# The convolution's layer norm and the first output products moved between the steps of the last pair of heads

## The chip, the cores and the metric

The kernel runs on one core of a Trainium2 chip. The metric is the device time of one launch in microseconds (us); the median of several runs counts. The profile is one more execution, taken by the hardware profiler.

## The reference

The program is two blocks on x of 512 tokens by 2048 channels, all in f32. Only the first half of the first block touches the change:

```python
u = rms_norm(h, norm_mix)
proj = u @ w_in                      # conv val, conv gate, r, k, v, three small ranks
y_conv = conformer_conv(val, gate, ...)   # val*sigmoid(gate), 31 causal taps, layer_norm over 1024, silu
y_rwkv = rwkv7_time_mix(...)         # 16 heads of 64, recurrent state, per-head norm, gate
mixed = concatenate([y_conv, y_rwkv])
h = h + mixed @ w_out                # 2048 x 2048
v = rms_norm(h, norm_ffn)
h = h + hierarchical_moe(v, ...)     # router, 32 experts, top 2
```

A second block (windowed attention beside a state-space layer) follows. Neither it nor the experts are edited.

## The kernel before

**Layout.** Activations lie transposed: 128 channels in the partitions, 512 tokens along the row. A "unit" is one product of 128 channels by 512 tokens. For the input projection a unit is 16 "steps", one matmul each over a block of 128 input channels (`DenseOne.step`). There are 43 of them, `N_IN`: one `lora`, two `rank`, and eight each of `val`, `gate`, `r`, `k` and `v`, in the order of `UNITS_ONE`, which is `FIRST` and then `LATER`. They take turns in two PSUM banks; a unit starts when ScalarE has evicted the one two before it. Weights come in panels of two units into a ring of two slots (`DenseOne.load`, on SyncE's queue SP).

**The pairs.** The time mix runs over eight pairs of heads, `pair(j)` on every engine. A pair has chunks of 64 tokens. TensorE makes masked scores, inverts a triangular system in five levels (`level_w`, `level_t`, each with an eviction on VectorE and copies on ScalarE between), forms the chunk transfers and then goes through six state steps. Its work is cut into 23 slots (`SLOTS_ONE`: A0 to A2, L0 to L4b for the levels, H, M, F, S1 to S6 for the state steps, and Y). Behind the small products of each slot TensorE takes as many projection steps as a table says: `FULL_SHARE` (sum 80) for pairs 0 to 5, `LAST_SHARE` (sum 64) for pair 6, none for pair 7. 9 units (`FIRST`) come ahead of pair 0. ScalarE evicts a finished unit in the same slot (`units(name)`), VectorE mixes it with the token before in the next one (`mix`), and GpSimd multiplies val by the gate (`gate_units`).

**The convolution.** VectorE takes a tile of 128 channels in 32 instructions (31 taps and one addition). How many of them stand in each slot is in `CONV_SHARE`, for each tile that the pair has: one tile in pairs 1 to 5, tiles 5 and 6 in pair 6, tile 7 in pair 7.

**The norm and the output.** After pair 7 TensorE sums the eight tiles over channels with `ones` (L764), VectorE centres them (L1251), ScalarE squares (L942), TensorE sums the squares (L769), VectorE and ScalarE form the reciprocal root, VectorE scales (L956), ScalarE applies Silu with gain and bias (L947). Then come 16 output units of 8 matmuls each (`out_unit`, L263) with the convolution's half of `w_out`, four panels of four units (one unit for each block of 128 tokens), which VectorE adds to the rows of x. The last pair's own norm (`mean`, `centre`, `variance`, `var`, `flip_y`, `norm_y`, `finish_y`) lies between them, and `pair_done` reaches 8 when it is through. `Middle` follows: 16 units with the other half of `w_out` (L1414), whose panels are the "late" ones, and the router in the same loop. The experts' weights then stream through a ring of 16 chunks of 1 MB; seven chunks are asked for early.

**SyncE's queue, in order:** output panels 0 and 1; rows of x after all 43 units; `c_scaled`; late panels 0 and 1; output panel 2; the router's inputs and seven expert chunks after `pair_done`; output panel 3; late panels 2 and 3.

## Time and profile before

| | us |
|---|---|
| median of 3 runs (3897.91 to 3901.66) | 3897.92 |
| profiled execution | 3898.68 |
| its span | 3896.7 |

| stretch of the span, us | what runs |
|---|---|
| 41 to 174 | units ahead of pair 0 |
| 174 to 979 | pairs 0 to 6 |
| 979 to 1041 | pair 7 |
| 1041 to 1071 | the convolution's norm |
| 1071 to 1184 | 16 output units of the convolution's half |
| 1184 to 1338 | the other half of the output, the router |
| 1338 to 2320 | experts |
| 2320 to 3897 | the second block |

The span is the time from the first to the last instruction; the execution has 2.0 us more around it. "PEclk" or the granted clock is the share of TensorE's full 2.4 GHz that it was given: 1.00 is 2.4 GHz and 0.50 is 1.2 GHz. PE is TensorE, DVE VectorE, ACT ScalarE, POOL GpSimd, SP SyncE.

### The profile page before, as it was taken

How to read it: one execution, taken by the hardware profiler on the slowest of the kernel's cores; microseconds unless marked ns; L12 is line 12 of the kernel's file. 1: busy time of each engine (PE TensorE's matmuls, PEld its weight loads, DVE VectorE, ACT ScalarE, POOL GpSimd, SP SyncE). 2: the span in 40 equal slices, each digit the busy share in tenths (PEclk: the TensorE clock that was granted, in tenths of full speed). 3: DMA queues.
4: the chain of work that ended last, by engine and by line, in shares of the span. 5: the costliest groups of instructions: out<-in, count | busy, mean ns of one | idle time of the engine just before them, and what ended most of it. 6: DMA issues, size and time to landing. Idle time of an engine off the chain costs nothing. (4 is left out here: it accounts for less than half of the span.)

```text
span 3896.7 us, 48147 instructions
## 1 busy us (share of the span) xinstructions
PE 3577.4 (92%) x20413; PEld 2129.6 (55%) x20413; DVE 1256.8 (32%) x2316; ACT 537.0 (14%) x976; POOL 415.1 (11%) x404
## 2 busy tenths in 40 slices
PE   8999999999699887777777768999999999999999
PEld 4455555555445432232322227754446888888888
DVE  2325445457511200000000004436302355444442
ACT  2122221222201100000000004110011010331000
POOL 0000000000000000000000000003020000465511
PEclk9999999999899899999999989999999999999999
DMA  4211111220151499999999987322443322222432
GB/s 116 65 46 44 46 46 46 56 58 23 68 184 44 194 421 422 422 422 422 421 420 419 417 340 192 104 81 87 108 113 108 114 85 67 76 83 103 162 117 77
DMA packets 318685, 666.31 MB, mean 171 GB/s; under 512 B 42972, under 2 KB 227718, under 8 KB 265125
## 3 DMA queue, kind: packets, MB, share of 16 engines
q1 hardware_dynamic: 310693, 636.35, 44.9%
q0 software_dynamic: 7808, 27.28, 1.9%
q8 instruction: 143, 2.34, 0.2%
q14 instruction: 41, 0.34, 0.0%
HBM read 636.44 MB, written 43.91 MB: 175 GB/s over the span
## 5 line engine op out<-in xcount | busy, mean ns | idle before, releaser
L1781 PE MATMUL experts_run_bank<-whole_big 128*64 128x512 f32 x2048 | 491.3, 627 | 169.1 <-DMA whole_big<-in_expert_w_gate 100.8
L2304 PE MATMUL stream_bank<-whole_big 128*128 128x256 f32 x2912 | 638.4, 380 | 0.6 <-DVE whole_big L3406 0.6
L242 PE MATMUL first_bank<-whole_big 128*128 128x512 f32 x1344 | 637.0, 611 | 1.3 <-PEq L80 1.3
L2304 PEld LDWEIGHTS stream_bank<-whole_big 128*128 128x128 f32 x2912 | 551.6, 190 | 80.0 <-issue 3.7
L2209 PE MATMUL stream_bank<-whole_big 128*128 128x512 f32 x1024 | 443.9, 593 | 0.0
L1781 PEld LDWEIGHTS experts_run_bank<-whole_big 128*64 128x64 f32 x2048 | 169.8, 144 | 489.7 <-issue 489.5
L242 PEld LDWEIGHTS first_bank<-whole_big 128*128 128x128 f32 x1344 | 241.5, 191 | 263.8 <-issue 253.1
L2209 PEld LDWEIGHTS stream_bank<-whole_big 128*128 128x128 f32 x1024 | 193.0, 190 | 236.4 <-issue 235.9
L1801 PE MATMUL experts_run_bank<-whole_big 128*64 128x512 f32 x1024 | 230.0, 596 | 35.2 <-DMA whole_big<-in_expert_w_down 22.8
L1846 DVE TENSOR_TENSOR whole_big<-whole_big,experts_run_bank 128x512 f32<-128x512 f32 x16 | 11.0, 687 | 650.2 <-PE experts_run_bank L1781 650.2
L2355 DVE TENSOR_TENSOR whole_big<-stream_bank,whole_big 128x256 f32<-128x256 f32 x250 | 102.2, 422 | 330.8 <-PE stream_bank L2304 330.8
L2947 PE MATMUL stream_bank<-whole_big 128*128 128x256 f32 x896 | 193.5, 379 | 0.0
L2947 PEld LDWEIGHTS stream_bank<-whole_big 128*128 128x128 f32 x896 | 170.2, 190 | 23.1
L1801 PEld LDWEIGHTS experts_run_bank<-whole_big 128*64 128x64 f32 x1024 | 79.1, 137 | 175.0 <-issue 167.1
L1022 DVE SCALAR_TENSOR_TENSOR whole_big<-whole_big 128x512 f32<-128x512 f32 x232 | 174.1, 785 | 0.2
L956 DVE TENSOR_TENSOR whole_big<-first_bank,whole_big 128x512 f32<-128x512 f32 x88 | 59.2, 688 | 291.1 <-PE first_bank L563 163.8
L956 DVE TENSOR_TENSOR whole_big<-whole_big 128x512 f32<-128x512 f32 (+3 forms) x158 | 113.2, 743 | 103.9 <-ACT whole_big L797 41.2
L263 PE MATMUL first_bank<-whole_big 128*128 128x512 f32 x256 | 112.8, 603 | 10.5 <-ACT whole_big L947 10.5
L1289 POOL TENSOR_TENSOR whole_big<-whole_big 128x512 f32<-128x512 f32 x40 | 54.5, 1375 | 634.1 <-DVE whole_big L956 491.0
L1414 PE MATMUL first_bank<-whole_big 128*128 128x512 f32 x256 | 113.4, 596 | 0.0
L2207 PE MATMUL stream_bank<-whole_big 128*128 128x256 f32 x512 | 111.7, 379 | 1.4 <-issue 1.4
L2207 PEld LDWEIGHTS stream_bank<-whole_big 128*128 128x128 f32 x512 | 96.7, 190 | 14.4 <-issue 1.6
(465 smaller groups left out, 3184.6 us busy)
## 6 DMA issues: line engine op xcount, KB each, us to landing
whole_big<-in_expert_w_gate SPq DMA_DIRECT2D x128, 1024.0 KB, 27.2
whole_big<-in_expert_w_up SPq DMA_DIRECT2D x128, 1024.0 KB, 30.0
whole_big<-in_expert_w_down SPq DMA_DIRECT2D x128, 1024.0 KB, 26.9
whole_big<-in_w_in SPq DMA_DIRECT2D x110, 1024.0 KB, 7.7
whole_big<-in_w_out SPq DMA_DIRECT2D x16, 1024.0 KB, 7.3
whole_big<-in_w_out SPq DMA_DIRECT2D x8, 2048.0 KB, 12.7
gates_two<-whole_big SPq DMA_DIRECT2D x40, 256.0 KB, 7.8
whole_big<-gates_two POOLq DMA_DIRECT2D x40, 256.0 KB, 3.0
```

The costliest lines, as they stand in the source:

```text
L242: mm = pe.matmul(bank[:, :], slot[:, k, sub * P:(sub + 1) * P], u_T[:, k, :], start=(k == 0), stop=(k == KD - 1))
L263: mm = pe.matmul(bank[:, :], mixed_T[:, k, token * P:(token + 1) * P], wide[:, k, :], start=(k == 0), stop=(k == 7))
L956: tt = lambda out, x, z, op: dve.tensor_tensor(out, x, z, op)
L1022: conv.did(dve.scalar_tensor_tensor(out=acc, in0=at, scalar=w, in1=acc, op0=ALU.mult, op1=ALU.add))
L1414: mm = pe.matmul(bank[:, :], self.mixed_T[:, 8 + k, t * P:(t + 1) * P], self.late[cb][:, k, :], start=(k == 0), stop=(k == 7))
L1781: mm = pe.matmul(bank[self.half(h), :], self.x_T[:, PARTS * q + k, self.half(h)], self.ring[slot][:, k, :], start=(q == 0 and k == 0), sto ...
L1801: mm = pe.matmul(self.y_bank[q][self.half(h), :], self.hidden_T[:, k, self.half(h)], self.ring[slot][:, q, :], start=(k == 0), stop=(k == ...
L2207: mm = pe.matmul(bank[:, 0:PW], left[:, k, t * P:(t + 1) * P], slot[:, k, :], start=(k == 0), stop=(k == KD - 1))
L2209: mm = pe.matmul(bank[:, :], slot[:, k, (u % 2) * P:(u % 2 + 1) * P], left[:, k, :], start=(k == 0), stop=(k == KD - 1))
L2304: mm = pe.matmul(self.place[m % 3], weights[:, k, :], left[:, k, :], start=(k == 0), stop=(k == self.k - 1))
L2355: ins = dve.tensor_tensor(to, bank, other, ALU.add)
L2947: mm = pe.matmul(out_place[q % 6], left[:, k, j * P:(j + 1) * P], right[:, k, :], start=(k == 0), stop=(k == 7))
```

## The change

- `FIRST` has one more unit, (val, 0): 10 units ahead of pair 0. The order in `LATER` is new: from pair 0 on, units finish as k, v, gate, val, r. All gates are through in pair 6's slot L2, v 7 in its S2. `LAST_SHARE` sums to 48.
- The convolution's tiles: 0 and 1 in pair 1, one each in pairs 2 to 5, 6 and 7 in pair 6, none in pair 7.
- In pair 7, `CLOSE_SHARE` says how many steps of a new kind (`close`) TensorE takes in each slot, 76 in all: 8 sum products in A0, 8 products of squares in L0 and L0b, and from L3 on 60 output matmuls, four in each slot and eight in Y. The other 68 output matmuls come after the pair.
- VectorE centres tiles in A1 and A2, forms variance in L0b and reciprocal in L1, scales in L1b and L2; ScalarE squares in A1 and L0, takes the root in L0b, and applies Silu in L2 and L2b. Both sums use the banks of the projection in place of R[0] and R[1], and there are three buffers for squares in place of two.
- VectorE adds output units 0 to 5 to the rows within the pair. The last pair's own norm lies between output units 7 to 11.
- SyncE: the rows of x after output panel 1 as before; output panel 2; then `c_scaled` and all of `y_mm`; late panels 0 and 1; output panel 3; then the router's inputs and the seven expert chunks.

```diff
-FIRST = [("lora", 0), ("rank", 0), ("rank", 1), ("r", 0), ("k", 0), ("v", 0), ("v", 1), ("r", 1), ("k", 1)]
...
+FIRST = [("lora", 0), ("rank", 0), ("rank", 1), ("r", 0), ("k", 0), ("v", 0), ("v", 1), ("r", 1), ("k", 1), ("val", 0)]
+LATER = [("gate", 0), ("val", 1), ("gate", 1), ("val", 2), ("r", 2)]
+LATER += [unit for j in range(2, 7) for unit in (("k", j), ("v", j), ("gate", j), ("val", j + 1), ("r", j + 1))]
+LATER += [("k", 7), ("gate", 7), ("v", 7)]
...
+SUM_U, VAR_U, OUT_U = N_IN, N_IN + 1, N_IN + 2
...
-LAST_SHARE = (5, 4, 4, 5, 5, 4, 5, 3, 2, 3, 2, 2, 2, 2, 2, 2, 1, 1, 1, 1, 1, 1, 6)
+LAST_SHARE = (5, 4, 4, 4, 4, 3, 4, 4, 3, 2, 2, 1, 1, 1, 1, 1, 2, 2, 0, 0, 0, 0, 0)
+CLOSE_SHARE = (8, 0, 0, 4, 4, 0, 0, 0, 0, 4, 4, 4, 4, 4, 4, 4, 4, 4, 4, 4, 4, 4, 8)
...
+CONV_CENTRES = {"A1": range(0, 4), "A2": range(4, 8)}
+CONV_SQUARES = {"A1": range(0, 3), "L0": range(3, 8)}
+CONV_VAR, CONV_ROOT, CONV_FLIP = "L0b", "L0b", "L1"
+CONV_SCALES = {"L1b": range(0, 4), "L2": range(4, 8)}
+CONV_SOFT = {"L2": range(0, 4), "L2b": range(4, 8)}
...
+    def out_step(self, pe, mixed_T):
+
+
+        u, k = self.at, self.k
         panel = panel_of_one(u)
-        slot, use, token = self.ring[panel % 2], panel // 2, (u - N_IN) % 4
+        slot, use, token = self.ring[panel % 2], panel // 2, (u - OUT_U) % 4
         wide = slot[:, :, :].rearrange("p (k two) c -> p k (two c)", two=2)
         bank = self.bank[u % 2]
-        pe.wait_ge(self.bank_free[u % 2], u // 2)
-        for k in range(8):
-            if token == 0 and k % 4 == 0:
-                pe.wait_ge(self.arrived[panel % 2][k // 4], 16 * use + 16)
-            mm = pe.matmul(bank[:, :], mixed_T[:, k, token * P:(token + 1) * P], wide[:, k, :], start=(k == 0), stop=(k == 7))
-        mm.then_inc(self.product, 1)
+        if k == 0:
+            self.open(pe, u)
+        if token == 0 and k % 4 == 0:
+            pe.wait_ge(self.arrived[panel % 2][k // 4], 16 * use + 16)
+        mm = pe.matmul(bank[:, :], mixed_T[:, k, token * P:(token + 1) * P], wide[:, k, :], start=(k == 0), stop=(k == 7))
+        self.k += 1
+        if self.k == 8:
+            mm.then_inc(self.product, 1)
+            self.at, self.k = u + 1, 0
...
-        squares = [kk, k2]
-        conv_var, conv_rstd = rate, e_inv
+        squares = [kk, k2, key_tmp]
+        conv_var, conv_rstd = rate, change
...
-                    if panel == PANELS_IN + 2:
-                        middle.sync_early(sp)
                     if panel == PANELS_IN + 1:
                         sp.wait_ge(dense.product, N_IN)
                         sp.dma_start(rows[:, :, :], a["x"][0].rearrange("(t p) d -> p t d", p=P)).then_inc(sem["rows_in"], 16)
+                    if panel == PANELS_IN + 2:
                         sp.wait_ge(sem["c_scaled"], CT)
+                        sp.wait_ge(sem["y_mm"], CT)
                         middle.sync_late(sp, 0)
                         middle.sync_late(sp, 1)
+                middle.sync_early(sp)
                 middle.sync(sp)
...
+                def close():
+
+
+                    n = closed[0]
+                    closed[0] = n + 1
+                    i = n % CT
+                    if n < CT:
+                        wait("conv", 32 * (n + 1))
+                        if i == 0:
+                            dense.open(pe, SUM_U)
+                        mm = pe.matmul(dense.bank[SUM_U % 2][:, :], ones[:, :], mixed_T[:, i, :], start=(i == 0), stop=(i == CT - 1))
+                        if i == CT - 1:
+                            mm.then_inc(dense.product, 1)
+                    elif n < 2 * CT:
+                        if i == 0:
+                            dense.open(pe, VAR_U)
+                        wait("c_sq", i + 1)
+                        mm = pe.matmul(dense.bank[VAR_U % 2][:, :], ones[:, :], squares[i % 3], start=(i == 0), stop=(i == CT - 1))
+                        mm.then_inc(*((sem["c_var_mm"], 1) if i < CT - 1 else (dense.product, 1)))
+                    else:
+                        if n == 2 * CT:
+                            dense.at = OUT_U
+                            wait("c_done", CT)
+                        dense.out_step(pe, mixed_T)
...
-                    after = share(j)
...
-                        dense.fill(pe, u_T, n)
+                        if more:
+                            dense.fill(pe, u_T, n)
+                        else:
+                            for _ in range(n):
+                                close()
...
+                dense.fill(pe, u_T, KD)
                 for j in range(CT):
                     pair(j)
-                wait("conv", 32 * CT)
-                wait("mt_ev", CT)
-                for i in range(CT):
-                    mm = pe.matmul(R[0][:, :], ones[:, :], mixed_T[:, i, :], start=(i == 0), stop=(i == CT - 1))
...
+                close_to(out_left + 1)
                 mean(CT - 1)
-                wait("c_done", CT)
-                for i in range(16):
-                    dense.out_unit(pe, N_IN + i, mixed_T)
-                    if i == 1:
-                        variance(CT - 1)
+                close_to(out_left + 3)
+                variance(CT - 1)
+                close_to(OUT_U + 16)
...
+                def square_conv(i):
+                    wait("c_centred", i + 1)
+                    if i >= 3:
+                        wait("c_var_mm", i - 2)
+                    act.activation(squares[i % 3], mixed_T[:, i, :], ACT.Square).then_inc(sem["c_sq"], 1)
+
+                def root_conv():
+                    wait("c_var", 1)
+                    act.activation(conv_var, conv_var, ACT.Sqrt).then_inc(sem["c_root"], 1)
+
+                def soft_conv(i):
+                    wait("c_scaled", i + 1)
+                    act.activation(mixed_T[:, i, :], mixed_T[:, i, :], ACT.Silu, bias=cols["conv_ln_b"][:, i:i + 1],
+                                   scale=cols["conv_ln_g"][:, i:i + 1]).then_inc(sem["c_done"], 1)
...
+                        if not more and name in CONV_SQUARES:
+                            for i in CONV_SQUARES[name]:
+                                square_conv(i)
+                        if not more and name in CONV_SOFT:
+                            for i in CONV_SOFT[name]:
+                                soft_conv(i)
+                        if not more and name == CONV_ROOT:
+                            root_conv()
...
+                def centre_conv(i):
+                    bank = dense.done(dve, SUM_U)
+                    ins = dve.scalar_tensor_tensor(out=mixed_T[:, i, :], in0=bank[:, :], scalar=-1.0 / n_conv, in1=mixed_T[:, i, :],
+                                                   op0=ALU.mult, op1=ALU.add)
+                    ins.then_inc(sem["c_centred"], 1)
+                    if i == CT - 1:
+                        wait("c_centred", CT)
+                        dve.sem_inc(dense.bank_free[SUM_U % 2], 1)
+
+                def var_conv():
+                    bank = dense.done(dve, VAR_U)
+                    dve.tensor_scalar(conv_var, bank[:, :], 1.0 / n_conv, 1e-5, ALU.mult, ALU.add).then_inc(sem["c_var"], 1)
+                    wait("c_var", 1)
+                    dve.sem_inc(dense.bank_free[VAR_U % 2], 1)
+
+                def flip_conv():
+                    wait("c_root", 1)
+                    dve.reciprocal(conv_rstd, conv_var).then_inc(sem["c_flipped"], 1)
+                    wait("c_flipped", 1)
+
+                def scale_conv(i):
+                    tt(mixed_T[:, i, :], mixed_T[:, i, :], conv_rstd, ALU.mult).then_inc(sem["c_scaled"], 1)
+
+                def add_row(i):
+                    bank = dense.done(dve, OUT_U + i)
+                    if i == 0:
+                        wait("rows_in", 16)
+                    at = rows[:, i % 4, (i // 4) * T:(i // 4 + 1) * T]
+                    tt(at, at, bank[:, :], ALU.add).then_inc(dense.bank_free[(OUT_U + i) % 2], 1)
...
-                    tiles = ([], [0], [1], [2], [3], [4], [5, 6], [7])[j]
+                    tiles = ([], [0, 1], [2], [3], [4], [5], [6, 7], [])[j]
...
+                        if more:
+                            return
+                        if i:
+                            for u in out_finished(i - 1):
+                                add_row(u)
+                        for k in CONV_CENTRES.get(name, ()):
+                            centre_conv(k)
+                        if name == CONV_VAR:
+                            var_conv()
+                        if name == CONV_FLIP:
+                            flip_conv()
+                        for k in CONV_SCALES.get(name, ()):
+                            scale_conv(k)
...
+                left = out_finished(len(SLOTS_ONE) - 1)[0]
+                for i in range(left, 16):
+                    if i == left + 1:
+                        centre(CT - 1)
+                    if i == left + 4:
                         var(CT - 1)
-                    if i == 4:
+                    if i == left + 5:
                         flip_y(CT - 1)
-                    if i == 5:
                         norm_y(CT - 1)
                         finish_y(CT - 1)
                         middle.vector_early(dve)
+                    add_row(i)
```

## Rows read from the trace of the kernel before

**Rows 1.** The page: busy time of each engine, and the group of the convolution's taps.

```profile
PE 3577.4 (92%) x20413; PEld 2129.6 (55%) x20413; DVE 1256.8 (32%) x2316; ACT 537.0 (14%) x976; POOL 415.1 (11%) x404
...
L1022 DVE SCALAR_TENSOR_TENSOR whole_big<-whole_big 128x512 f32<-128x512 f32 x232 | 174.1, 785 | 0.2
```

**Rows 2.** Stretches: length, busy PE, PEld, DVE, ACT, POOL; granted clock, DMA share, GB/s.

```profile
748.00:864.00 116.00, 116.00 (x1134) 62.39 (x1134) 58.84 (x82) 27.74 (x40) 7.95 (x6) 1.00 0.15 38
...
864.00:979.00 115.00, 110.81 (x1104) 60.17 (x1103) 78.39 (x114) 25.74 (x38) 8.45 (x6) 0.93 0.13 39
...
979.00:1041.00 62.00, 44.02 (x962) 38.70 (x960) 41.44 (x59) 13.06 (x21) 8.11 (x6) 0.84 0.27 103
...
1041.00:1071.00 30.00, 17.98 (x39) 6.88 (x36) 14.44 (x19) 13.61 (x20) 0.00 (x0) 0.84 0.02 2
...
1071.00:1184.00 113.00, 113.00 (x258) 49.77 (x258) 16.42 (x22) 2.09 (x3) 0.78 (x4) 0.98 0.44 161
...
1338.00:2320.00 982.00, 770.32 (x3392) 292.15 (x3392) 73.43 (x112) 39.50 (x65) 36.72 (x61) 0.96 0.99 412
```

**Rows 3.** Waits of TensorE, 864 to 1184 us: total, times, longest.

```profile
PE first_bank L590 <- DVE whole_big L956: 12.4, 4, 4.5
...
PE first_bank L263 <- ACT whole_big L947: 10.5, 1, 10.5
...
PE first_bank L734 <- DVE whole_big L1124: 6.9, 9, 1.3
```

**Rows 4.** Timeline of TensorE: start, duration, what, records.

```profile
159.31 13.89 PE L242 MATMUL first_bank<-whole_big 128*128 128x512 f32 x32
...
382.56 1.98 PE L242 MATMUL first_bank<-whole_big 128*128 128x512 f32 x4
...
403.40 1.15 PE L563 MATMUL first_bank<-whole_big 64*64 64x64 f32 x32
...
865.64 1.15 PE L563 MATMUL first_bank<-whole_big 64*64 64x64 f32 x32
...
974.77 4.68 PE L242 MATMUL first_bank<-whole_big 128*128 128x512 f32 x8
...
979.37 2.36 PE L563 MATMUL first_bank<-whole_big 64*64 64x64 f32 x64
...
990.81 1.97 PE L590 MATMUL first_bank<-whole_big 64*64 64x64 f32 x32 [4.55 <-DVE whole_big L956]
...
1087.90 96.29 PE L263 MATMUL first_bank<-whole_big 128*128 128x512 f32 x224
...
1184.03 6.17 PE L1414 MATMUL first_bank<-whole_big 128*128 128x512 f32 x14
```

**Rows 5.** Timeline of VectorE in pair 6.

```profile
905.89 1.29 DVE L956 TENSOR_TENSOR whole_big<-first_bank,whole_big 128x512 f32<-128x512 f32 x2 [4.38 <-PE first_bank L563]
...
932.62 0.69 DVE L956 TENSOR_TENSOR whole_big<-first_bank,whole_big 128x512 f32<-128x512 f32 x1 [1.70 <-PE first_bank L579]
...
949.65 0.23 DVE L1121 COPY whole_big<-first_bank 128x64 f32<-128x64 f32 x1 [1.36 <-PE first_bank L724]
...
963.64 0.28 DVE L1124 SCALAR_TENSOR_TENSOR whole_big<-whole_big,first_bank 128x64 f32<-128x64 f32 x1
```

**Rows 6.** Stretches of 4 us, columns as in rows 2.

```profile
960.00:964.00 4.00, 3.67 (x11) 1.58 (x12) 4.00 (x10) 0.00 (x0) 0.00 (x0) 0.50 0.00 0
...
1044.00:1048.00 4.00, 4.00 (x9) 1.75 (x9) 0.00 (x0) 0.00 (x0) 0.00 (x0) 0.87 0.00 0
```

**Rows 7.** Timeline of VectorE and ScalarE in the norm.

```profile
1060.80 3.35 DVE L1256 RECIPROCAL whole_big<-whole_big 128x512 f32<-128x512 f32 x1 [0.69 <-ACT whole_big L944]
...
1064.18 4.92 DVE L956 TENSOR_TENSOR whole_big<-whole_big 128x512 f32<-128x512 f32 x8
...
1064.91 5.75 ACT L947 ACTIVATE whole_big<-whole_big,whole_one 128x512 f32<-128x512 f32 x8 [2.85 <-DVE whole_big L956]
```

**Rows 8.** Timeline of SP's queue.

```profile
1118.74 0.37 SPq L1380 DMA_DIRECT2D whole_big<-in_router_group_w  x1
```

More of the change, by code:

```diff
@@ L156, in finished, with out_finished @@
     return range(done // KD, (done + share(j)[slot]) // KD)
+def out_finished(slot):
+    done = sum(CLOSE_SHARE[:slot]) - 2 * CT
+    return range(max(done, 0) // 8, max(done + CLOSE_SHARE[slot], 0) // 8)
 def panel_of_one(u):
-    return 0 if u < 2 else 1 + (u - 3) // 2 if u < N_IN else 1 + (N_IN - 3) // 2 + (u - N_IN) // 4
+    return 0 if u < 2 else 1 + (u - 3) // 2 if u < N_IN else 1 + (N_IN - 3) // 2 + (u - OUT_U) // 4
+CONV_CENTRES = {"A1": range(0, 4), "A2": range(4, 8)}
[3 more added lines that the diff above has]
+CONV_SOFT = {"L2": range(0, 4), "L2b": range(4, 8)}
 PANELS_IN = panel_of_one(N_IN - 1) + 1
@@ L517, in _ @@
                     dense.load(sp, panel)
-                    if nearest < CT and panel < PANELS_IN and dense.last(panel - 2) >= len(FIRST) + 5 * (nearest - 2) + 3:
+                    if nearest < CT and panel < PANELS_IN and dense.last(panel - 2) >= len(FIRST) + 5 * (nearest - 2) + 2:
                         load_up(nearest)
                         nearest += 1
-                    if panel == PANELS_IN + 2:
-                        middle.sync_early(sp)
                     if panel == PANELS_IN + 1:
@@ L603, in variance @@
                     pe.matmul(R[5][:, :], block_ones[:, :], tmp, start=True, stop=True).then_inc(sem["var_mm"], 1)
+                closed = [0]
+                def close():
[20 more added lines that the diff above has]
+                        dense.out_step(pe, mixed_T)
                 def pair(j):
                     more = j < CT - 1
-                    after = share(j)
+                    after = share(j) if more else CLOSE_SHARE
                     spent = {}
@@ L758, in _, with close_to @@
                 bonus_sum(0)
+                dense.fill(pe, u_T, KD)
                 for j in range(CT):
                     pair(j)
[L761 to L776 removed]
+                def close_to(u):
+                    while dense.at < u:
+                        close()
+                close_to(out_left + 1)
+                mean(CT - 1)
+                close_to(out_left + 3)
+                variance(CT - 1)
+                close_to(OUT_U + 16)
                 wait("pair_done", CT)
@@ L1365, in unit @@
     def unit(self, i):
-        return N_IN + 16 + i
+        return OUT_U + 16 + i
     def sync_late(self, sp, i):
@@ L1387, in sync @@
         sem, dense = self.sem, self.dense
-        sp.wait_ge(dense.product, N_IN + 12)
+        sp.wait_ge(dense.product, OUT_U + 12)
         self.sync_late(sp, 2)
-        sp.wait_ge(dense.product, N_IN + 16)
+        sp.wait_ge(dense.product, OUT_U + 16)
         self.sync_late(sp, 3)
@@ L1682, in gpsimd @@
                            pattern=[[1, P]], channel_multiplier=-1).then_inc(sem["counted"], 1)
-        pool.wait_ge(self.dense.product, N_IN + 32)
+        pool.wait_ge(self.dense.product, OUT_U + 32)
         pool.memset(self.expert.x, 0.0).then_inc(sem["x_clear"], 1)
```

55 lines of the change are left out of this document (9 added, 46 removed).

## Prediction

> **What bounds the kernel now.** I read the page first: TensorE is busy 92% of the span, so what can be won is its idle time and the time it spends at half clock [rows 1]. The table of stretches then says where that is [rows 2]. From 748 to 864 us (the pair of heads before the last two) TensorE is busy 116.00 of 116.00 us at a granted clock of 1.00 (2.4 GHz). The trouble lies in 864 to 1071: pair 6 is at clock 0.93; the last pair (979 to 1041) is busy for 44.02 of 62.00 us at 0.84; in the convolution's norm (1041 to 1071) it is busy 17.98 of 30.00. The output products behind (1071 to 1184) are full again. The waits of TensorE from 864 to 1184 name the causes [rows 3]: 12.4 us for VectorE's evictions of the levels, 10.5 for ScalarE's Silu before the first output product, 6.9 for VectorE's state steps. So up to 1184 TensorE's own order sets the time. Behind it come the router and then the experts, which move 412 GB/s at a DMA share of 0.99 [rows 2]; that stream waits for ring slots which TensorE's first expert products free, so what TensorE wins before it starts, the stream wins too.
>
> **Prices.** A matmul of 512 columns is two records: 16 projection steps took 13.89 us back to back (from 159.31), 0.87 each, and 112 output steps took 96.1 us (1087.90 to 1184.03), 0.86 each [rows 4]. Four whole pairs from 403.40 to 865.64 give 115.6 us each. Of that 80 steps take 69.6 and the small products 46.0; the last pair lacks the next pair's ranks and sums (about 6), so its own work is 39.3 us at full clock. It lasted 61.7 (from 979.37 to just behind 1041), and from its start to the router's first product (1184.03) it is 204.7 us.
>
> **Part 1: one more projection unit ahead of pair 0** (FIRST has 10 units): +13.9 us. Nothing hides it: TensorE had no wait there to fill. The sizes for pairs 0 to 5 stay at 80 steps each, only the kinds of unit change places. The gates now come at L4b, each with a table load on ScalarE; it falls into the time of the fill, cost 0.
>
> **Part 2: pair 1 takes two convolution tiles instead of one.** Pair 6 shows what two tiles do: VectorE is busy 78.39 us of 115, against 58.84 of 116 with one tile in pair 5 [rows 2]. With full fills that fits everywhere but in the six state steps: VectorE needs 14.0 us for them with two tiles (949.65 to 963.64 [rows 5]), 2.3 each, and TensorE's own rhythm there is 2.2, two fills of 1.98 (from 382.56 [rows 4]) and 0.2 of small products. I take +1 us; the bounds are 0 and 5 (a spell at half clock).
>
> **Part 3: pair 6 has 48 fills instead of 64.** 16 steps are 13.9 us if TensorE sets the pace. It doesn't throughout. Up to the rb/rk masks (905.89) VectorE has idle time, and three steps fewer bring them 2.7 us forward. From there to the first state copy (949.65) VectorE idles 1.70 us before 932.62, 1.36 before 949.65 and little else in 43.8 [rows 5]. The last eviction of the levels (932.62) comes 3.2 us sooner; then 13.1 us of VectorE work, two taps and the q sum stand in a row, and state copy 0 comes 4.6 us sooner where TensorE alone would give 7.0. The six state steps are VectorE's (949.65 to 963.64 with no idle), and the mixing of v 7 now stands among them, +1.3: the last is 3.3 sooner. Then the six fills of slot Y are gone: they ran at or near half clock, 2.0 for each of two and 4.6 for the last four (from 974.77) [rows 4, 6], less 0.6 for waits that they covered. Together -11.4 us (period 102.3). Bounds: -7 and -14.5.
>
> **Part 4: the last pair and the norm.** Taken away: the 32 taps in it, 25 us at 0.785 each [rows 1], and the serial norm behind it. Added between its steps: 8 sum products, 8 variance products, 60 output steps. I count from the pair's start. The clock is half there, since waits in the state steps bring it down (before: 0.50 from 960 on [rows 6]). Scores 4.0, sum products 9.9 (about 4 us of them at half clock, as the norm's sum needed, which began at 1041: 0.87 from 1044 on [rows 6]): 13.9. Turns, scores, y's mean and level 0's product: 18.4. VectorE has meanwhile 8 centrings at 0.61 (as its 8 scalings took [rows 7]), a mask, y's centring and the eviction: 20.8, hidden by 4 variance products (21.9). Squaring 2.2, turns 1.0, y's variance 1.0, four more variance products with 0.3 of waiting for squares: 29.9. Level 1 with 1.0 of wait: 34.2. Scores and level 2's product: 38.1. Here comes the wait that takes the place of the old one: VectorE does the norm's reciprocal (3.35) to 35.3, the masks to 38.3, y's reciprocal (3.35), four scalings at 0.61 and the eviction, until 44.7. TensorE waits 6.7 us with nothing to fill (L1b has share 0); before, the longest such wait was 4.5 [rows 3]. Then 4.4 of products to 49.3, and ScalarE has four Silus left after X's copy (0.72 each [rows 7]) until 51.9; output steps wait for all eight, so 2.7 more: 52.1. From L3 on every slot has 4 steps, which cover everything (in pairs 0 to 5, 2 to 4 steps did). Left: own work 16.6 and 60 steps at 0.86, 51.5: 120.2. Behind: 68 steps 58.3, y's mean and variance 2.0: 180.5. After the two long waits I add 4.0 for half clock, for behind the old wait of 4.55 us (990.81) 32 small products took 1.97 us instead of the 1.1 of full clock, and the rest of their run with them [rows 4]. 184.5 against 204.7: -20.2 us. Bounds: no half clock and half the waits, 171; half clock to L3, 203.
>
> **Part 5: the queues.** SP asks for x's rows when the 43 units are done, now in pair 6; for output panel 2 four units into the output; then it waits for y_mm of the last pair, asks for late panels 0 and 1 (4 MB, 10 us at the experts' 412 GB/s), needed 8.5 units, 58 us, later. Output panel 3 stands behind them, needed 28 us after its slot frees. Router inputs and seven expert chunks come after pair_done, which falls some 28 us before the output ends (before 66, at 1118.74 [rows 8]). The chunks are 7.3 MB, 18 us; late panel 2 stands behind them and lands about when the output ends, 14 us before its use; late panel 3 is asked for as before. The router's weights have some 40 us. Cost 0; without that cover, the late panel would cost what exceeds 14.
>
> **Sum.** 13.9 + 1 - 11.4 - 20.2 = -16.7 us. The profiled execution took 3898.7 (span 3896.7, 2.0 around it), 0.8 above the median of 3897.9; 3897.9 - 16.7 = 3881.2, so 3881.
>
> **The rivals.**
> (B) The waits are smaller than walked: pair 6 sheds all 16 steps (-14.0), pair 1 costs nothing, the 9.4 us of new waits halve and no half clock follows them (-28.9): 13.9 - 14.0 - 28.9 = -29, 3870. For it: I took each engine's work as coming in one piece after its last input, where some of it can start sooner. Against: two reciprocals and the masks in a row on VectorE between level 1 and level 2.
> (C) VectorE sets pair 6: it has 79.7 us of work and the levels' round trips, and sheds 3 us instead of 11.4. The unit moved ahead is paid twice: 3881 + 8.4 = 3889 to 3890. For it: the full row of VectorE's work before the state steps [rows 5]. Against: the Y fills stand behind that work.
> (D) Slower: half clock holds on in the last pair. At 960 it fell to 0.50 though TensorE was busy 3.67 of 4.00 us, with single steps between small products [rows 6], and the last pair still began near it. In the new last pair, slots A1 to L2b are small products between waits. At half clock up to L3 its 37 us of work cost up to 19 more than I counted: 3900. It decides whether the clock is still half where L3 begins, for then the slots L3 to H (34 us of work) run so too: 3930, slower. Against: in the row from 1044 it was back at 0.87, some 4 us after dense products began, and the sum products are dense, as are the runs of four steps from L3 on. The Trainium skill (TensorE: Matmul & The Clock Gate, "HAM oscillation — how this bites in real kernels") says that waits between short bursts of matmuls bring the clock down again and again; the fall in the row at 960 agrees. By that rule alone each of the two new waits would be followed by a cold stretch, and the kernel would come out near 3900.
> (E) The change wins on TensorE but not at the end: late panel 2, the router's weights or x's rows arrive late and give back what was won, 3893 to 3898. Against: the margins of part 5.
>
> **How the numbers follow.** A (as summed, 3874 to 3889) 0.55; B 0.20; C 0.12; D 0.06; E 0.07. The bound for "no change" is 0.2%, 7.8 us, which is about what a measurement of this kernel can tell: below 3890.1 is faster. That takes A, B and 0.05 of C: 0.80; same 0.14; slower 0.06. The range 3865 to 3893 leaves out D, E and the edge of B.
>
> **What would show it.** Pair 0 starts at about 188 instead of 174. Pair 6 lasts about 102 us, with TensorE waiting for state steps longer than before (6.9 us with the last pair's [rows 3]). The last pair starts near 983 and ends near 1103; its longest wait is a level-2 eviction of 6 to 7 us, and there is none before the output products but 3 us for Silu. The router's first product comes at about 1167 instead of 1184, and from there every stage is as long as before. I am wrong if pair 6 lasts over 106 us (C), if the clock of the last pair before L3 is under 0.7 (D), or if the way from 1184 to the first expert product (154 us) has grown (E).

## The result and the profile after

| | before | after |
|---|---|---|
| median, us | 3897.92 (5 runs, 3892.96 to 3901.66) | 3877.25 (5 runs, 3875.67 to 3880.40) |
| ratio, 95% interval | | 0.9950 (0.9937 to 0.9963) |
| profiled execution, span | 3898.68, 3896.7 | 3875.67, 3873.9 |

The change makes the kernel 20.7 us faster, where -16.7 was forecast; 3877 lies in the range of 3865 to 3893. In a second job, with six runs, the changed kernel gave 3878.2, ratio 0.9954 (0.9943 to 0.9966).

The page of the changed kernel: busy time, and the group of the output steps (L283, before L263), whose waits were 10.5 us in [rows 3].

```profile
PE 3567.3 (92%) x20413; PEld 2123.0 (55%) x20413; DVE 1263.4 (33%) x2316; ACT 539.1 (14%) x978; POOL 419.0 (11%) x404
...
L283 PE MATMUL first_bank<-whole_big 128*128 128x512 f32 x256 | 116.4, 605 | 2.6 <-ACT whole_big L911 2.6
```

The stretches, columns as in rows 2: pair 1 with two tiles, pair 6, the last pair with what is between its steps, the experts.

```profile
283.00:399.00 116.00, 115.91 (x1134) 62.38 (x1133) 75.00 (x106) 26.46 (x39) 8.05 (x6) 1.00 0.16 42
...
877.00:978.00 101.00, 90.17 (x1061) 53.02 (x1062) 80.89 (x116) 23.75 (x36) 9.03 (x6) 0.93 0.20 75
978.00:1099.00 121.00, 111.21 (x1121) 64.00 (x1118) 37.40 (x52) 24.31 (x39) 6.76 (x5) 0.92 0.09 30
...
1315.00:2297.00 982.00, 769.61 (x3392) 292.67 (x3392) 73.43 (x112) 39.50 (x65) 36.56 (x61) 0.96 0.99 412
```

Pair 1 is still busy 115.91 of 116 us. Pair 6 is 101 us long and not 115, but TensorE is busy only 90.17 of them. The separate stretch for the norm is gone. The experts' 982 us are as long as before [rows 2], so what was won ahead of them stayed won.

The timeline of TensorE: the unit ahead of pair 0, the starts of pair 0, pair 6 and the last pair, its sum products and what follows them, the two long waits and the router's first product.

```profile
171.32 13.89 PE L255 MATMUL first_bank<-whole_big 128*128 128x512 f32 x32
185.15 1.15 PE L588 MATMUL first_bank<-whole_big 64*64 64x64 f32 x32
...
876.97 1.15 PE L588 MATMUL first_bank<-whole_big 64*64 64x64 f32 x32
...
978.24 0.36 PE L588 MATMUL first_bank<-whole_big 64*64 64x64 f32 x1
...
984.20 8.23 PE L642 MATMUL first_bank<-whole_big,whole_ones 128*128 128x512 f32 x14
992.27 1.04 PE L593 MATMUL first_bank<-whole_ident,whole_big 128*128 128x128 f32 x8
...
1021.08 1.97 PE L615 MATMUL first_bank<-whole_big 64*64 64x64 f32 x32 [6.27 <-DVE whole_big L1019]
...
1029.69 5.10 PE L283 MATMUL first_bank<-whole_big 128*128 128x512 f32 x8 [2.58 <-ACT whole_big L911]
...
1161.29 13.90 PE L1506 MATMUL first_bank<-whole_big 128*128 128x512 f32 x32
```

| from, to | before [rows 4] | after | difference | forecast |
|---|---|---|---|---|
| extra unit ahead of pair 0 | | 13.83 (171.32 to 185.15) | +13.8 | +13.9 |
| pair 0 to pair 6 | 691.65 | 691.82 | +0.2 | +1 |
| pair 6 to last pair | 113.73 | 101.27 | -12.5 | -11.4 |
| last pair to router | 204.66 | 183.05 | -21.6 | -20.2 |
| sum | | | -20.1 | -16.7 |

The router's first product comes 22.7 us sooner, since another 2.6 us lie in the opening, which the change doesn't touch. Of the runs of 32 transposes there, the second took this long before and after (timeline of TensorE in each kernel):

```profile
20.43 5.47 PE L418 MATMUL opening_bank<-whole_big 128*128 128x128 f32 x32 [1.84 <-DVE whole_big L388]
```

```profile
19.48 3.84 PE L441 MATMUL opening_bank<-whole_big 128*128 128x128 f32 x32 [1.84 <-DVE whole_big L411]
```

In the twelve further profiles below, all of kernels that are the same as the changed one up to there, pair 0 starts between 185.16 and 187.96 us. So the difference is chance of one execution. The end has such chance too: from the experts' first product to the end of the span, the changed kernel took 2558.1 us in this profile (from 1315.85 to 3873.9) and 2562.3 in its second one (after_again). So what follows is read from the stretches and not from the span, and medians that differ by some 4 us or less are not told apart by themselves.

The waits of TensorE from 877 to 1160 us; L615 is the eviction wait of the levels and L790 that of the state steps, in rows 3 L590 and L734 (1.1 us more for a state copy stand at y's first product, L798):

```profile
PE first_bank L615 <- DVE whole_big L1019: 7.1, 2, 6.3
PE first_bank L790 <- DVE whole_big L1219: 6.7, 3, 3.8
PE first_bank L790 <- DVE whole_big L1216: 2.9, 1, 2.9
PE first_bank L283 <- ACT whole_big L911: 2.6, 1, 2.6
```

The long one, 6.27 us at level 2 (1021.08), is VectorE's work in a row. In its timeline the norm's reciprocal (1009.50), the two masks, y's reciprocal, four scalings and then the eviction (1020.35) follow with one pause, 0.68 us for the masks' scores:

```profile
1009.50 3.34 DVE L1191 RECIPROCAL whole_big<-whole_big 128x512 f32<-128x512 f32 x1
1013.53 1.29 DVE L1019 TENSOR_TENSOR whole_big<-first_bank,whole_big 128x512 f32<-128x512 f32 x2 [0.68 <-PE first_bank L588]
1014.74 3.34 DVE L1159 RECIPROCAL whole_big<-whole_big 128x512 f32<-128x512 f32 x1
1018.00 2.43 DVE L1019 TENSOR_TENSOR whole_big<-whole_big 128x512 f32<-128x512 f32 x4
1020.35 0.68 DVE L1019 TENSOR_TENSOR whole_big<-first_bank,whole_big 128x512 f32<-128x512 f32 x1
```

The clock around the pair's start, columns as in rows 6. It was 0.50 from 968 to 988 though TensorE was busy nearly all the time from 976 on; it was back once the sum products (from 984.20) had run for some 4 us:

```profile
972.00:976.00 4.00, 3.19 (x54) 3.03 (x55) 3.97 (x8) 0.00 (x0) 0.00 (x0) 0.50 1.00 414
976.00:980.00 4.00, 3.94 (x75) 3.75 (x73) 0.65 (x1) 0.60 (x1) 0.00 (x0) 0.50 1.02 424
...
984.00:988.00 4.00, 4.00 (x11) 1.82 (x8) 3.87 (x5) 0.00 (x0) 2.95 (x2) 0.50 0.00 0
988.00:992.00 4.00, 4.00 (x10) 1.77 (x10) 0.56 (x1) 0.00 (x0) 0.00 (x0) 0.98 0.00 0
```

SP's queue: late panels 0 and 1, output panel 3, then the router's inputs at 1133.70. No wait of TensorE for a transfer appears in the waits above.

```profile
1096.12 2.19 SPq L1465 DMA_DIRECT2D whole_big<-in_w_out  x4
1104.83 0.92 SPq L231 DMA_DIRECT2D whole_big<-in_w_out  x2
1133.70 0.37 SPq L1472 DMA_DIRECT2D whole_big<-in_router_group_w  x1
```

### The profile page after: what moved, and what is told of

Its sections match the earlier page's. It is cut to its first block and busy times, and to the rows that moved or that the text cites. A ratio compares the mean times of both kernels' runs of the same rounds, so it can differ in the third digit from the quotient of the medians.

```text
span 3873.9 us, 48151 instructions
## 1 busy us (share of the span) xinstructions
PE 3567.3 (92%) x20413; PEld 2123.0 (55%) x20413; DVE 1263.4 (33%) x2316; ACT 539.1 (14%) x978; POOL 419.0 (11%) x404
## 5 line engine op out<-in xcount | busy, mean ns | idle before, releaser
L283 PE MATMUL first_bank<-whole_big 128*128 128x512 f32 x256 | 116.4, 605 | 2.6 <-ACT whole_big L911 2.6
```

The costliest lines, as they stand in the source:

```text
L283: mm = pe.matmul(bank[:, :], mixed_T[:, k, token * P:(token + 1) * P], wide[:, k, :], start=(k == 0), stop=(k == 7))
```

## The experiments

All ratios are to the kernel before in the same job, whose median was 3896.9 to 3899.3 us from job to job. "Pair 6" and "last" are the stretches of the table above in each kernel's own profile.

| kernel | median | ratio, 95% interval | pair 6 | last |
|---|---|---|---|---|
| before | 3897.9 | | 113.7 | 204.7 |
| the changed kernel | 3877.3 | 0.9950 (0.9937 to 0.9963) | 101.3 | 183.1 |
| after_again | 3878.2 | 0.9954 (0.9943 to 0.9966) | 101.3 | 184.6 |
| norm_in_outputs_behind | 3881.4 | 0.9961 (0.9946 to 0.9976) | 101.3 | 185.7 |
| norm_behind_no_taps | 3897.6 | 0.9997 (0.9988 to 1.0007) | 101.4 | 199.7 |
| early_back | 3909.2 | 1.0035 (1.0023 to 1.0046) | 101.3 | 212.7 |
| taps_in_y | 3875.7 | 0.9946 (0.9933 to 0.9959) | 97.4 | 181.1 |
| flip_later | 3874.8 | 0.9937 (0.9924 to 0.9951) | 101.3 | 179.4 |
| warm_steps | 3869.7 | 0.9931 (0.9917 to 0.9944) | 99.0 | 178.7 |
| taps_and_flip | 3871.2 | 0.9927 (0.9914 to 0.9941) | 97.5 | 179.1 |
| warm_steps_flip | 3869.4 | 0.9922 (0.9908 to 0.9935) | 99.2 | 176.8 |
| warm_all_flip | 3866.4 | 0.9921 (0.9907 to 0.9934) | 99.0 | 172.8 |
| warm_all_taps_flip | 3859.5 | 0.9899 (0.9884 to 0.9914) | 93.6 | 172.8 |
| warm_router_too | 3863.0 | 0.9915 (0.9902 to 0.9929) | 93.6 | 172.8 |

**The changed kernel again.** 

> The changed kernel once more, beside the others on the same chip. From the two traces the gain is made of +13.8 us (unit ahead of pair 0), about 0 (pairs 0 to 5), -12.5 (pair 6), -21.6 (last pair to the router), together -20; another 2.6 us of the profiled difference lay in the opening, where one of the two executions had its transposes at half clock for longer. If the opening is chance, the ratio of times is 0.9945 to 0.9952 and the new trace may have either opening; if the change causes the earlier start, every trace of the changed kernel starts pair 0 at 185 us and the gain is 22 to 23.

The ratio, 0.9954, is just outside the 0.9945 to 0.9952 that was expected if the opening is chance, by far less than its interval, and pair 0 started at 187.56 us instead of 185.15. The opening's first four runs of transposes took 6.54, 5.46, 5.46 and 3.84 us, as in the kernel before (6.43, 5.47, 5.47 and 3.84), where the first profile of the changed kernel had 5.25, 3.84, 5.47 and 3.84: it is chance. The last pair's stretch differs by 1.5 us between the two profiles of the same kernel. The spell of half clock behind the wait for Silu is longer in the second one: the granted clock was 0.50 and 0.73 in its two rows from 1032 to 1040 us, and 0.93 and 1.00 in those of the first.

**The outputs behind the pair, the norm within.**

```diff
-CLOSE_SHARE = (8, 0, 0, 4, 4, 0, 0, 0, 0, 4, 4, 4, 4, 4, 4, 4, 4, 4, 4, 4, 4, 4, 8)
+CLOSE_SHARE = (8, 0, 0, 4, 4) + (0,) * 18
...
-                left = out_finished(len(SLOTS_ONE) - 1)[0]
+                left = 0
```

> The 16 sum and variance products stay in the last pair, the 60 output steps go behind it. If the steps in slots L3 to S6 cover waits and keep the clock up, their waits come back as in the kernel before (about 5 us for levels and state steps behind the 2.6 us for Silu) and so does the half clock from the state steps on (some 15 us of it before, 7 lost): slower than the changed kernel by 9 to 13 us, 3886 to 3890. If the norm's place alone makes the gain and the output steps only change places, it is within 3 us of the changed kernel.

A miss. The stretch is 185.7 us, 1.1 to 2.6 longer than in the two profiles of the changed kernel, and the median 3 to 4 higher. The waits do come back, 5.4 us of them behind level 2's eviction, about as expected, and half clock too. But the wait of 2.6 us for Silu is gone, since no output step stands right behind the Silus any more. In its timeline a wait for a level's eviction is 0.80 us, one for a state copy 0.38, and from 1044 on the small products run at half clock (0.48 for four):

```profile
1028.65 1.15 PE L615 MATMUL first_bank<-whole_big 64*64 64x64 f32 x32 [0.80 <-DVE whole_big L1019]
...
1042.68 0.33 PE L790 MATMUL first_bank<-whole_big 64*64 64x64 f32 x4 [0.38 <-DVE whole_big L1219]
...
1048.47 0.48 PE L798 MATMUL first_bank<-whole_big 64*64 64x64 f32 x4
```

So the output steps had only some 3 us net to cover, and a spell of half clock. Against that, the changed kernel starts a run of output steps in each of 14 slots, and each start costs about 0.2 us (eight records take 3.70 us alone, and 3.5 in a long run), an estimated 3 us. This balance is worked out from the traces; no run changes one part of it alone.

**The norm behind the pair too.**

```diff
-CLOSE_SHARE = (8, 0, 0, 4, 4, 0, 0, 0, 0, 4, 4, 4, 4, 4, 4, 4, 4, 4, 4, 4, 4, 4, 8)
+CLOSE_SHARE = (0,) * 23
...
-CONV_CENTRES = {"A1": range(0, 4), "A2": range(4, 8)}
...
+CONV_CENTRES, CONV_SQUARES, CONV_SCALES, CONV_SOFT = {}, {}, {}, {}
+CONV_VAR = CONV_ROOT = CONV_FLIP = None
...
+                for i in range(CT):
+                    centre_conv(i)
+                var_conv()
+                flip_conv()
+                for i in range(CT):
+                    scale_conv(i)
+                left = 0
```

(ScalarE's squares, root and Silus move behind the pair in the same way.)

> Units, tiles and queue as in the changed kernel, but the sum and variance products, the whole norm and all output steps stand behind the last pair. From the pair's start to the router it was 204.7 us before, 183 to 185 after, and 185.7 with only the outputs behind. If the norm's place makes the gain, this kernel pays its serial chain again (26 to 28 us from the pair's end to the first output step) and takes back only the taps that left the last pair (some 12 us of its 62, since the waits for levels and state steps shrink): 192 to 196 us, 3885 to 3891 in all. If the gain came mostly from the taps' departure, it is under 190.

199.7 us, above the 192 to 196 expected, and the whole gain is gone (0.9997). The wait for Silu is back, longer than in [rows 3]:

```profile
PE first_bank L280 <- ACT whole_big L908: 11.3, 1, 11.3
```

With this one the 21.6 us split: 204.7 to 199.7 by the taps leaving the last pair (4.9), 199.7 to 185.7 by the norm between its steps (14.1), 185.7 to 183.1 or 184.6 by the output steps (1.1 to 2.6). The parts were taken in this one order; in another they could share out otherwise. I had expected the taps to give 12.

**Router inputs and expert chunks ahead of output panel 3.**

```diff
                 for panel in range(2, PANELS_IN + 4):
+                    if panel == PANELS_IN + 3:
+                        middle.sync_early(sp)
                     dense.load(sp, panel)
...
-                middle.sync_early(sp)
                 middle.sync(sp)
```

> Router inputs and seven expert chunks are asked for ahead of output panel 3 again, as in the kernel before. In the changed kernel pair_done comes when output unit 12, the first of panel 3, is about to start (1133.7 us). If the order of the queue matters, panel 3 is asked for only then and stands behind 7.3 MB: unit 12 waits 18 to 26 us, 3895 to 3903. If the transfers of several requests run side by side and share the rate, or if the wait is taken back in front of the experts, it costs under 10 us.

The order of the queue matters, and more than expected. TensorE waits 27.4 us for the panel, and the kernel is 31 us slower than the changed one and slower than before. The first reason is that SP itself needs 8 us from the first small request to the panel's, and the second that the panel, asked for at 1144.30, lands at 1163.85 behind 7.3 MB.

```profile
PE first_bank L283 <- DMA whole_big<-in_w_out: 27.4, 1, 27.4
```

```profile
1136.17 0.37 SPq L1473 DMA_DIRECT2D whole_big<-in_router_group_w  x1
...
1144.30 4.21 SPq L231 DMA_DIRECT2D whole_big<-in_w_out  x2
```

So the new order of requests earns nothing that these runs show, but with the output products moved it is needed: before, `pair_done` came at 1118 [rows 8], with more than half of the output units still ahead; now it comes when panel 3 is about to be used.

**16 taps of pair 6 in slot Y of pair 5.**

```diff
+LAST_TAPS = (0, 5, 0, 2, 3, 3, 0, 3, 2, 2, 4, 2, 2, 6, 2, 2, 1, 1, 1, 1, 1, 1, 4)
...
-                        for _ in tiles:
-                            k = (conv.n + 0) // 32
-                            n = CONV_SHARE[i]
+                        counts = [CONV_SHARE[i]] * len(tiles) if j != 6 else [LAST_TAPS[i]]
+                        if j == 5 and name == "Y":
+                            counts.append(16)
+                        for n in counts:
```

> 16 of the 64 taps of pair 6 are done in slot Y of pair 5, where VectorE is idle for some 14 us; six of them come out of the slots before L2b, ten out of those behind, six of these from the state steps. If VectorE sets pair 6 from level 2 to the last state step, as the trace says (TensorE waits 10.7 us there for state copies), pair 6 shortens by 6 to 9 us and the kernel by as much: 3868 to 3871. If the round trips between the engines set it and not VectorE's work, under 2 us.

Between the two: pair 6 is 3.9 us shorter, not 6 to 9, and against 0.9950 and 0.9954 the ratio of 0.9946 is no difference that this measurement can tell. The waits for state copies fell from 10.7 to 7.0 us (below, with 0.5 at y's first product); up to the first state step the pair lost only 0.9 us, from 80.4 to 79.4, though eight taps had left that part and VectorE's busy time in it had fallen by 5.5 us, from 61.3 to 55.8. So VectorE sets the state steps, but the levels of pair 6 seem to be set by both engines in turn. The last stretch, 181.1 us, is shorter too, by 2.0 to 3.5.

```profile
PE first_bank L792 <- DVE whole_big L1221: 4.5, 3, 3.1
PE first_bank L792 <- DVE whole_big L1218: 2.0, 1, 2.0
```

**y's reciprocal behind level 2's eviction.**

```diff
-                    if j:
+                    if j and more:
                         flip_y(j - 1)
...
-                    if j:
+                    if j and more:
                         norm_y(j - 1)
                     rest("L2")
+                    if not more:
+                        flip_y(j - 1)
+                        norm_y(j - 1)
```

> In the last pair the reciprocal and norm of the pair before (y) come behind level 2's eviction and the scalings, no longer ahead of it. The walk through the pair says that the wait at level 2 (6.3 us) is VectorE's serial work between two handoffs, of which this reciprocal is 3.35: the wait falls to about 3, the Silu wait stays at 2.6, and the half clock behind the wait shortens: 3 to 6 us faster than the changed kernel. If the wait had another cause (the masks' scores, or the copies of ScalarE), nothing changes; if the Silus set the start of L3 anyway, the gain is taken back by a longer wait there.

The stretch is 3.7 to 5.2 us shorter and the median 2.4 to 3.4 lower: the reciprocal was part of the wait. The wait fell to 4.2 and not to 3, and that for Silu stayed, as expected.

```profile
PE first_bank L615 <- DVE whole_big L1019: 4.9, 2, 4.2
PE first_bank L283 <- ACT whole_big L911: 2.6, 1, 2.6
```

**Unused matmuls in pair 6's waits.** They read finished data, and their sums are never used; the output is unchanged.

```diff
                         fill(f"S{c}")
+                        if j == CT - 2:
+                            for _ in range({3: 1, 4: 4, 5: 1, 6: 1}.get(c, 0)):
+                                pe.matmul(R[4][:, :], block_ones[:, :], K_in[1][:, 1:1 + T], start=True, stop=True)
```

> Seven matmuls of 512 columns whose results nobody uses stand in slots S3 to S6 of pair 6, where TensorE waits for state copies. They are extra work, 6.1 us at full clock, laid into 7.8 us of waits. If half clock is what makes the end of pair 6 and the start of the last pair slow (0.50 from 968 to 988 us), the clock stays near 1.00 and y's products, scores and the first sum products get some 6 to 8 us back: 3869 to 3873. If the clock doesn't follow from these waits, or falls anyway, the kernel is the same or up to 3 us slower.

As the first case of the expectation says. TensorE has 14 more instructions (two records for each matmul), and the kernel is faster: the two stretches are 6.6 to 8.2 us shorter together, and the median 7.5 to 8.5 lower, though the intervals of the ratios overlap. The clock is 1.00 in each row where it was 0.50 above (columns as in rows 6), and the waits are filled:

```profile
968.00:972.00 4.00, 3.12 (x14) 1.09 (x14) 4.00 (x8) 0.00 (x0) 0.00 (x0) 1.00 1.06 408
...
976.00:980.00 4.00, 4.00 (x91) 3.06 (x87) 1.60 (x3) 0.60 (x1) 0.00 (x0) 1.00 1.01 418
...
984.00:988.00 4.00, 3.93 (x45) 2.56 (x43) 2.44 (x5) 1.59 (x4) 0.00 (x0) 1.00 0.02 4
```

```profile
PE first_bank L790 <- DVE whole_big L1219: 2.9, 1, 2.9
PE first_bank L790 <- DVE whole_big L1222: 0.9, 2, 0.7
```

Pair 6 is 2.2 us shorter (y's products at full clock), and the last pair 4.4 to 5.9. Its scores and sum products show it directly: they took 14.03 us in the changed kernel (978.24 to 992.27), and 9.38 here, from 976.39 to the next line:

```profile
985.77 1.04 PE L593 MATMUL first_bank<-whole_ident,whole_big 128*128 128x128 f32 x8
```

**Both rearrangements.** The edits of taps_in_y and flip_later.

> Both rearrangements, taps in Y and the later reciprocal, in one kernel. They act in different pairs, so the gains add: 9 to 14 us on the changed kernel, 3863 to 3868. If either gain only moves TensorE's wait to the other place, the sum is that of one.

3871.2, 6 to 7 us under the changed kernel, less than the 9 to 14 expected. In the trace the gains don't add fully: 97.5 for pair 6 as with the taps alone, and 179.1 for the rest, as with the later reciprocal alone. The 2.0 to 3.5 us by which the taps alone had shortened the last stretch don't come on top; why, wasn't tried.

**The later reciprocal and the unused matmuls.** The edits of flip_later and warm_steps.

> The seven unused matmuls in pair 6 and the later reciprocal in the last pair. Alone they gave 2.3 us in pair 6 with 4.4 to 6 from the last pair's start, and 3.6 in the last pair. They act on different waits: the last pair to the router takes 175 to 176 us against 183 to 185, the kernel 3865 to 3867.

The stretch is 176.8, somewhat more than the 175 to 176 expected and a further 1.8 us under warm_steps; the median (3869.4, 3865.6 to 3870.3) can't be told from that of warm_steps alone. Against flip_later, which differs only by the seven unused matmuls, the two stretches are 2.1 and 2.5 us shorter and the median is 5.4 lower.

**Unused matmuls in the last pair's waits as well.** `warm(n)` issues n such matmuls; two stand behind F of pair 6, four ahead of level 2's squaring and two ahead of the first output step.

```diff
                     fill("L2")
+                    if not more:
+                        wait("var", j)
+                    warm(4, CT - 1, R[5])
...
+                    warm(2, CT - 1, R[5])
                     fill("L3")
...
                     fill("F")
+                    warm(2, CT - 2, R[4])
```

> In addition unused matmuls of 512 columns in F of pair 6 (2), and in the last pair four at level 2's wait (4.2 us with the later reciprocal) and two at the wait for Silu (2.6). They don't shorten a wait; they only keep TensorE busy in it. If half clock behind each wait is a cost of its own (0.50 to 0.87 over some 8 us there), 3 to 4 us faster than warm_steps_flip: 3862 to 3864. If those short spells cost nothing, equal or up to 2 us slower.

The last stretch is 4.0 us shorter, the median 3.0; the intervals of the two kernels overlap. From 975 to 1025 us the granted clock was 0.91 without them and is 1.00 with them (the stretch in warm_steps_flip, then in warm_all_flip):

```profile
975.00:1025.00 50.00, 42.32 (x656) 30.01 (x652) 34.50 (x42) 20.23 (x32) 7.17 (x5) 0.91 0.17 69
```

```profile
975.00:1025.00 50.00, 47.82 (x685) 30.73 (x680) 32.59 (x39) 21.42 (x34) 7.17 (x5) 1.00 0.10 39
```

**The same with the taps in slot Y.**

> The same with 16 taps of pair 6 in slot Y of pair 5 and fewer unused matmuls to fit the shorter waits. Taps gave 3.8 us in pair 6, waits and not clock, so it should add: 3858 to 3862. If pair 6's end is set by TensorE once its clock is full, the taps bring under 1 us more.

3859.5, in the expected range: the best of all kernels here, 39.5 us under the kernel before and some 18 under the changed one. Pair 6 is 5.4 us shorter than in warm_all_flip (93.6 against 99.0), more than the 3.9 of the taps alone.

**And in the router's last waits.** Ten more unused matmuls, three ahead of the last rank product, one ahead of the last spread, six ahead of the wait for the overflow table.

```diff
         logit(15)
+        warm(3)
         rank(TT - 1)
+        warm(1)
         spread(TT - 1)
...
+        warm(6)
         pe.wait_ge(sem["over_ready"], 1)
```

> warm_all_taps_flip with ten more unused matmuls of 512 columns behind the router's last products, where TensorE waits 2.8, 1.3 and 6.2 us for VectorE and the clock is 0.50 from 1280 to 1300 us until the first expert products have run 2 to 3 us. If half clock costs there as it did behind the pairs, the small products and the first expert's turns (3.7 us for 16) run at full clock: 1 to 4 us faster, 3855 to 3858. If the chain there is VectorE's, so that only the first expert's turns gain, or if the matmuls come in the way of the products that VectorE waits for, within 1 us or slower.

Not borne out. From the router's first product to the experts' first turns it is 1.5 us shorter (153.1 against 154.5), but those turns still run at half clock, since a wait of 4.2 us for the barrier between the stages lies ahead of them, and the median is 3.5 us higher. First warm_all_taps_flip, then this kernel:

```profile
1292.64 1.89 PE L1585 MATMUL first_bank<-whole_big 128*64 128x15 f32 x16 [6.19 <-DVE whole_big L1737]
1298.19 3.89 PE L1874 MATMUL experts_run_bank<-whole_ident,whole_big 128*128 128x128 f32 x16 [3.66 <-PEq L80]
```

```profile
1293.43 1.10 PE L1592 MATMUL first_bank<-whole_big 128*64 128x15 f32 x16 [1.78 <-DVE whole_big L1744]
1298.77 3.89 PE L1881 MATMUL experts_run_bank<-whole_ident,whole_big 128*128 128x128 f32 x16 [4.23 <-PEq L80]
```

Pair 6 and the last stretch are as in warm_all_taps_flip. In the profiles the longer time lies in the opening (pair 0 at 187.5 instead of 185.4) and behind the experts' start (2562.5 us to the end instead of 2559.1). Both differences are as large between the two profiles of the changed kernel, and the two medians come from different jobs. So the record shows neither a gain nor a loss of these ten matmuls in the whole time.

## Why the prediction was right

**Part 1** (+13.9): 13.83, nothing hid it. **Part 2** (+1): 0.2 over all six pairs; two tiles fit under full fills.

**Part 3** (-11.4): -12.5. Its steps hold in the main, one by one: the first state copy came 4.0 us sooner (4.6 said), the last 2.6 (3.3 said), and from there to the pair's end 5.9 us instead of 15.7, 9.8 shorter where 8.1 was said. Slot Y's six fills were sized rightly: from y's first product to the pair's end it took 14.2 us before and 5.5 after, 8.7 less, against 2.0 + 2.0 + 4.6 in the sum. The sum left out the fill of state step 6, which stood between the last state copy (963.64) and y's first product, 1.52 us later; after the change that product starts 0.42 us behind the last copy (972.34). And the 0.6 us that it took off for covered waits was not lost. Before, then after:

```profile
963.15 2.07 PE L242 MATMUL first_bank<-whole_big 128*128 128x512 f32 x2
965.16 0.49 PE L742 MATMUL first_bank<-whole_big 64*64 64x64 f32 x4
```

```profile
972.76 0.48 PE L798 MATMUL first_bank<-whole_big 64*64 64x64 f32 x4 [1.13 <-DVE whole_big L1219]
```

taps_in_y suggests that the picture of VectorE alone as the limit holds only for the state steps. The reading of rows 5 behind that picture also passed over an idle time of VectorE of 1.19 us before a level's eviction at 921.88.

**Part 4** (-20.2): -21.6 and -20.1 in two profiles. The walk from the pair's start gave 13.9 us to the end of the sum products (14.0 measured), a wait of 6.7 at level 2 (6.27), one of 2.7 at Silu (2.58), and 52.1 to L3 (51.45). Half clock was of the right size in both places: the walk's 13.9 us for scores and sum products were 9.38 at full clock in warm_steps, and behind the waits, where 4.0 was added, warm_all_flip won 4.0. What the sum didn't say is which edit earns it. The output products between the steps, 60 matmuls in 14 slots, bring 1.1 to 2.6; the norm's place 14.1; the taps' departure 4.9. Had the prediction been for the output products alone, I would have put it several times too high, as the expectation for norm_in_outputs_behind did.

**Part 5** (0): no transfer was waited for up to the experts, and from the router's first product to the experts' first it took 154.6 us before and after. early_back shows the margin that the order of requests buys: 27 us.

**The sum** was 4 us short of the medians' difference. The stretches of the profiles account for -18.6 to -20.1 of it, against -16.7; the rest is within the spread of both kernels' runs. Small slips of its arithmetic don't matter here: 44.7 and 4.4 give 49.1 and not 49.3, and B's sum gives 3869 and not 3870.

**The rivals.** (C) fell: pair 6 shed 12.5 us, not 3. (D) fell: the clock came back some 4 us after the sum products had begun to run close together, each long wait was followed by a short spell only (0.50 in the row from 1020, 0.64 in that from 1028, 1.00 in that from 1036), and up to L3 the last pair's granted clock was 0.83, where under 0.7 would have been its sign. The Trainium skill (TensorE: Matmul & The Clock Gate, "HAM oscillation — how this bites in real kernels") says that waits between bursts bring the clock down again and again. The trace agrees in the row at 972 (0.50) and behind both waits, though the waits here are for other engines and not for transfers as in that section's case. What this costs in this kernel, some 5 us at the pair's start and 4 behind the waits, could be bought back with useless work. (E) fell, as part 5 says. (B) was the nearest of them: the median lies between A's 3881 and B's 3870, but no wait was half as long as walked.

## What to carry to other kernels

A serial chain through three engines (here a norm over partitions) costs little once it stands between the steps of other work: here it gave two thirds of the last stretch's gain, while moving bulk products between the later steps gave about a tenth, since few waits were left to cover. Moving work forward can be repaid only if the place it came from isn't limited by another engine, so ask which engine limits each slot, and move requests in a queue along with the point at which their condition is met. Where TensorE must wait, look at the clock behind the wait before shortening the wait; filling it paid at the pairs, and not ahead of the barrier between the router and the experts.

## What the runs showed of the hardware

Seven matmuls of 512 columns whose results nobody reads, laid into the waits between the state steps of pair 6, made pair 6 and the stretch behind it 6.6 to 8.2 us shorter: they bring no state copy sooner, but the granted clock stayed at 1.00 where it had been 0.50 for 20 us. Eight more, in the waits of the last pair and in slot F of pair 6, won another 4.0 us in the trace.

At half clock TensorE can look fully busy: it was busy 3.94 to 4.00 us of every 4 from 976 to 988 at a granted clock of 0.50. Busy time alone hides this loss.

The opening differs from execution to execution: the same 32 transposes took 5.47 or 3.84 us, and pair 0 started up to 2.8 us apart in kernels that are the same up to there.
